# Value products of an attention loop held back for four steps, in front of the ones

## The reference, cut to what matters

```python
h = x @ w_in                                   # x (8, 2048, 1024)
qa, ka, va, za, qb, kb, vb, zb, ga, gb = jnp.split(h, IN_OFFSETS, axis=-1)
ya = windowed_sink_attention(qa, ka, va, sink_a)   # |t - s| <= 128
ya = (ya * silu(za)) @ w_proj_a
qh, kh = rope(rms_norm(qb)), rope(rms_norm(kb))
p  = softmax(qh @ kh.T * 64 ** -0.5)               # over all 2048 keys
yb = ((p @ vb) * silu(zb)) @ w_proj_b
y  = (sigmoid(ga + b_a) * ya + sigmoid(gb + b_b) * yb) @ w_out
out = layer_norm(2 ** 0.25 * x + y)
```

## Time and profile before

| | |
|---|---|
| median of 3 runs | 691.49 us (691.06 to 768.03) |
| the profiled execution | 690.76 us, its span on the slowest core 688.5 us |
| spans of the eight cores | 674.2 to 688.5 us |
| TensorE busy on the slowest core | 612.4 us (89%) |
| ScalarE, VectorE, GpSimdE busy | 407.4, 323.9, 121.0 us |
| TensorE's mean granted clock, cores 0 to 7 | 0.977 to 0.991 |

### The profile page before, as it was taken

The page is one execution under the profiler, slowest core; times in us unless marked ns, Lnnn a source line. Parts: engine busy times, 40 slices in busy tenths (PEclk is TensorE's granted clock), DMA queues, the critical chain, the costliest instruction groups (busy, mean ns, idle before and its releaser), DMA issues.

```text
span 688.5 us, 12484 instructions; the slowest of 8 cores (674.2 to 688.5 us)
## 1 busy us (share of the span) xinstructions
PE 612.4 (89%) x3761; PEld 217.6 (32%) x3832; DVE 323.9 (47%) x564; ACT 407.4 (59%) x545; POOL 121.0 (18%) x189
## 2 busy tenths in 40 slices
PE   3789879998789999999999999999997899969982
PEld 1356522223223233333333333333322223323430
DVE  2198821224424243436647333456733323693477
ACT  0156579874486767677666767676765777502200
POOL 3268550101002100111111011111010111012011
PEclk9999989999899999999999999999999999999997
DMA  8979749644115543454465545445771342245202
GB/s 137 150 119 122 93 64 157 104 138 59 53 32 75 127 75 66 78 79 90 96 142 139 122 63 94 63 74 114 192 201 38 63 94 45 68 152 101 52 30 92
DMA packets 44817, 66.33 MB, mean 96 GB/s; under 512 B 16976, under 2 KB 19152, under 8 KB 44496
## 3 DMA queue, kind: packets, MB, share of 16 engines
q0 software_dynamic: 21232, 38.31, 36.8%
q1 hardware_dynamic: 23520, 27.22, 13.7%
HBM read 95.04 MB, written 8.52 MB: 150 GB/s over the span
## 4 chain that ended last, share of the span: by engine, by line
PE 64%; issue 9%; DVE 9%; ACT 8%; DMA 7%; SPq 1%; DVEq 0%; ACTq 0%; POOL 0%; POOLq 0%
PE PS L257 64%; ACT PT L266 4%; DMA SZ<-ws 2%; DVE SS L386 2%; ACT WR L266 1%; DMA D<-R 1%; SPq L276 1%; DVE QB L272 1%; DMA XT<-xT 1%; DVE WR L269 1%; DMA out<-T 1%; DVE STT L567 1%; DVE T L272 1%; ACT G L266 1%; DVE QA L272 1%
## 5 line engine op out<-in xcount | busy, mean ns | idle before, releaser
L266 ACT ACTIVATE PT<-PS 128x1024 bf16<-128x1024 f32 (+1 forms) x304 | 295.0, 1018 | 112.1 <-PE PS L257 110.3
L257 PE MATMUL PS<-XT,WROT 128*128 128x512 bf16 x857 | 218.0, 386 | 11.2 <-issue 4.0
L257 PEld LDWEIGHTS PS<-XT,WROT 128*128 128x128 bf16 x896 | 77.5, 98 | 135.1 <-issue 64.1
L276 POOL DMA_DIRECT2D WROT<-wg x100 | 53.5, 537 | 349.1 <-PE PS L257 347.9
L257 PE MATMUL PS<-PT,VX 128*64 128x512 bf16 (+3 forms) x688 | 100.9, 370 | 13.3 <-DVE O L269 9.2
L272 DVE SCALAR_TENSOR_TENSOR G<-G,PS 128x512 f32<-128x512 f32 x64 | 43.4, 686 | 112.5 <-PE PS L257 98.3
L257 PE MATMUL PS<-QB,KB 64*128 64x512 bf16 x512 | 82.6, 386 | 7.9 <-ACT PT L266 6.1
L266 ACT ACTIVATE G<-PS,CVH 128x512 f32<-128x512 f32 x64 | 44.1, 688 | 62.9 <-PE PS L257 62.0
L257 PE MATMUL PS<-SZ,XT 128*128 128x384 bf16 (+1 forms) x249 | 56.3, 370 | 16.3 <-DMA XT<-xT 15.1
L257 PE MATMUL PS<-SZ,WR 128*128 128x512 bf16 x243 | 64.2, 380 | 5.1 <-ACT G L266 2.2
L257 PE MATMUL PS<-WR,T 128*128 128x512 bf16 x244 | 59.5, 380 | 5.7 <-DVE QB L272 2.8
(11 more groups left out here) (62 smaller groups left out, 382.6 us busy)
## 6 DMA issues: line engine op xcount, KB each, us to landing
WROT<-wg POOLq DMA_DIRECT2D x100, 256.0 KB, 6.0
R<-den SPq DMA_DIRECT2D x64, 128.0 KB
T<-x SPq DMA_DIRECT2D x8, 512.0 KB
out<-T SPq DMA_DIRECT2D x8, 512.0 KB
QB<-x SPq DMA_DIRECT2D x6, 512.0 KB
out<-QB SPq DMA_DIRECT2D x6, 512.0 KB
SZ<-ws POOLq DMA_DIRECT2D x8, 256.0 KB, 8.8
XT<-xT POOLq DMA_DIRECT2D x2, 1024.0 KB, 9.6
```

What stands on the lines that cost most here:

```text
L257: s.op("pe", lambda e: e.matmul(out, lhsT=lhsT, rhs=rhs, start=start, stop=stop, skip_group_check=skip), reads=reads, writes=writes)
L266: s.op("act", lambda e: e.activation(out=out, in_=in_, func=func, **kw), reads=reads, writes=writes)
L276: s.op(eng, lambda e: e.dma_start(out=out, in_=in_), reads=reads, writes=writes, dma=True)
```

## The change

The value products of a batch are no longer issued in their own pass. They are held back with the ones: when four steps are owed, or the item ends, the value products of all owed steps are issued, and then all their ones. What is computed, the order of the sums within a bank and all other operations stay as they are.

```diff
         for i, (w, bt) in enumerate(all_b):
             if i + 1 < len(all_b):
                 start_batch(all_b[i + 1][1])
-            for st in bt:
-                st.pv()
             owed.extend(bt)
             if len(owed) == 4 or bt[-1].last:
+                for st in owed:
+                    st.pv()
                 for st in owed:
                     st.ones()
                 owed.clear()
```

## The result

The changed kernel takes 699.7 us (median of four runs, 698.4 to 699.8) against 692.1; the ratio is 1.011, with a 95% interval from 1.009 to 1.013. It is slower by a little over 1%, about 8 us. The forecast was 691, no change. The time lies in the wide range of 682 to 701, but above the 683 to 698 that the forecast's own terms allow, and the kernel moved where no movement was forecast.

The account below looks back on a forecast made before the run. TensorE was taken as the bound, with ScalarE's 2.94 us floor between issues and V's waits on VectorE. The terms 11.8 - 3.5 - 9.1 + 1 = +0.2 us gave 691 us, 683 to 698 by single terms, wide range 682 to 701.

Parts of the forecast that it names:

- Step 1: TensorE's changes between matmul kinds: one fewer per global (B) group, -0.11 us; two fewer per window (A) item, -0.22 us.
- step 2: Global (B) groups: without V as cover, ScalarE's 2.94 us floor makes S to the ones at least 3.92 us; together +11.8 us.
- step 5: Hidden effects: fill tiles ending earlier wait more for a free bank, +1 us, bounds 0 and +5; the other effects 0.
- step 3: Window (A) items: two changes of kind less in 16 items, -3.5 us; one exponential under 2 us of fill does not bind.
- Step 4: V's waits for VectorE shrink because V comes one or two batches later: -9.1 us, bounds -2 and -17.
- the wait at 515 us: V's largest wait, 3.79 us behind VectorE's late small DMA: -2.4 us, and -1.5 for clock that a shorter wait may spare.
- The small waits: V's short waits on VectorE: four for `O` go, -2.2 us; half of the short ones for `PT`, -1.0 us.
- the A items of the first window: Two `O` waits of 1.59 us and a `PT` wait of 1.55 at 166 to 185 us: -2.0 us, bounds 0 and -8.
- ScalarE starting later than 0.54 after S: Rival: a tanh before the exponentials raises the floor about 0.2 us in 48 first batches, +10, 701 us; chance 0.2.
- The clock: Rival: 48 new short TensorE gaps make the clock swing in the attention loop, +25, 716 us; chance 0.03.
- The sign: Whole kernel: terms cancel to +0.2 us, no change; past the 2% bound, chance 0.03 faster and 0.09 slower.

Follow-up runs that it names:

- hold_a: Changed kernel, but value products held back only in the three-step window (A) items, issued at once in global (B) items: 690.4 us, ratio 0.997.
- after_half: Changed kernel with the exponential of one head only, half of the exponentials left out: 675.3 us, one execution.
- before_half: Kernel before the change with the exponential of one head only, half of the exponentials left out: 683.2 us, one execution.
- after_x3: Changed kernel with the loads of x from the fourth on issued on GpSimd's queue instead of SyncE's: ratio 1.002 to the kernel before.
- before_x3: Kernel before the change with the loads of x from the fourth on issued on GpSimd's queue instead of SyncE's: ratio 0.990.
- after_rec: Changed kernel with an item's reciprocal, its spread and last multiplication done two passes later: median 697.3 us, ratio 1.007 to the kernel before.
- after_xpool: Changed kernel with all loads of x issued on GpSimd's queue instead of SyncE's: ratio 1.0025 to the kernel before.

## Why the prediction was wrong

- **Step 1, changes of kind: right.** 0.11 for S to F in the first timeline; `hold_a`'s w1 is 0.9 shorter for four A items, and `after_half`'s 2.9 shorter than `before_half`'s.
- **Steps 2 and 3, B groups and A items: right.** 2.94 and 3.92 to a hundredth, in every window. With the long stall out of both kernels the B items came out at +12.9 us, where step 2 said 11.8 and step 5 another 1 for bank waits, and the A items at -3.6, where step 3 said -3.5. The segments add up to +9.2, where the steps without relief said 11.8 - 3.5 + 1 = 9.3.
- **Step 4, V's waits: this is the step that failed.** -9.1 was forecast, bounds -2 and -17. In the pair without the long stall next to nothing of it came (9.2 against 9.3), and the original pair lies as far apart. The `O` waits did fall (9.2 to 0.7), but a wait that falls isn't a gain. The largest term, -2.4 and -1.5 of clock, is the wait at 515 us. I had put "five fill matmuls and the next S" in front of V, as if they could run. They need banks that VectorE drains, and VectorE was the engine that stood. The trace of the kernel before had it, behind the last line of the earlier trace rows, though the prediction shows no such line: `G` had the next place in VectorE's stream behind `O`.

```profile
518.78 0.69 DVE L269 TENSOR_TENSOR O<-PS,SZ 128x512 f32<-128x512 f32 x1
519.39 0.68 DVE L272 SCALAR_TENSOR_TENSOR G<-G,PS 128x512 f32<-128x512 f32 x1
```

After the change two of the five ran, three waited 6.15 us, and the clock fell all the same. w3 went from 127.6 to 132.1 us on the worst core and from 124.9 to 132.1 on the profiled ones; its price without the stall is 3.8 (`after_x3` less `before_x3`), so no relief is left in either. The median's +6.7 is that price and a stall that more cores met. The small waits (-2.2 and -1.0) gave nothing that shows in the segments either. For the A items of the first window I took -2.0. The profiled core did gain 2.9 there (35.7 to 32.8), but it had by far the longest A0-A3 of the eight, and the medians came out at -0.1: V's waits for `O` fell from 3.0 to 0.5, and in their place those for `PT` and for VectorE's other work grew from 1.8 to 3.5. `after_rec`, which takes VectorE's wait away, shows that 2.7 us were to be had.
- **Step 5, +1 for bank waits:** 3.1 to 5.3 us of waits for `G` where none is long (before and `after_x3`), so some 2 us, inside the bounds.
- **The rivals.** ScalarE starting later than 0.54 after S did not happen in the groups of the changed kernel shown; the slower outcome came with the forecast's own floor. That 699.7 lies inside 682 to 701 is luck: the room above 698 was given to this rival. The clock: 1.00 from 188 to 207 us with six waits of some 0.5 us, and 1.00 through the middle windows. The Trainium skill's rule (TensorE: Matmul & The Clock Gate, A second HAM failure mode) did not show itself for gaps of this size.
- **The sign.** Two terms of nine microseconds stood against each other, one read from a repeating row in some 50 places, the other from a handful of stalls on one core of one execution. The sum of the two was not "no change" but "+9, less something uncertain", and the chance of a slower kernel should have said so.

The tail after the last ones was 1.8 us shorter on the slowest core (89.5 to 87.7). Both lengths stand in both profiles, one core of eight near 88 before and six after; why was not tried.

## What to carry to other kernels

Before work is moved out of a place, ask what was hidden under it: here V stood where TensorE had to wait for ScalarE anyway, and a minimum distance between two issues (2.94 us) was readable from one repeating row. With other work of the same length put into the gap, the reordered kernel was 1.5% faster than the one before. And when an in-order engine stalls on a DMA, everything that it owes is late; moving one of its customers behind others helps only if those others don't need it too.

## What was not expected of the hardware

- A 4 KB transfer issued right behind a 512 KB load on SyncE's queue was waited for until 12 us after its issue (512.46 to 524.44); with the load on GpSimd's queue the long stall in the last window was gone on all eight cores of `after_xpool`. Whether the place in the queue or the load on the DMA engines (88% busy in the last 6.5 us) made it late was not separated: the edit also lets the load start at another time.
- Eight 64-column matmuls in a run cost what two runs of four cost, less one change of kind: 0.98 against 2 x 0.55. No weight load shows in that time.
- The price of a change of kind, about 0.11 us, was the same for S to F, which the kernel before never did, as for all others.
